# Cross-attention values for all heads at once, memory rows on partitions, and a reordered opening in a two-layer trunk

## The reference, cut to what matters

```
h = rms_norm(x, attn_norm_w[i]); proj = h @ w_in[i]      # xq: 4 heads x 128; cq: 512; gates ...
mh = rms_norm(mem, mem_norm_w[i])
mk, mv = jnp.split(mh @ w_mem_kv[i], 2, axis=-1)         # (256, 4 x 128) each
sc = einsum('bqhd,bkhd->bhqk', xq, mk) * 128 ** -0.5
pc = softmax(sc, axis=-1)
co = einsum('bhqk,bkhd->bqhd', pc, mv)
```

## Time and profile before

| | us |
|---|---|
| median of 3 runs (lowest, highest) | 1961.29 (1961.13, 1962.27) |
| the profiled execution, its own time | 1960.48 |
| its span in the profile | 1958.7 |
| TensorE matmul busy | 1946.5 (99%) |
| GpSimd busy | 1067.7 (55%) |
| VectorE busy | 1038.8 (53%) |
| ScalarE busy | 928.4 (47%) |

### The profile page before, as it was taken

One profiled execution on the slowest core, in us unless ns is written; L12 is line 12 of the kernel. 1 busy time (PEld: TensorE's weight loads), 2 busy tenths in 40 slices (PEclk: granted clock), 3 DMA queues, 4 the chain that ended last, 5 costly groups with the idle time before them and its releaser, 6 DMA issues.

```text
span 1958.7 us, 28631 instructions
## 1 busy us (share of the span) xinstructions
PE 1946.5 (99%) x9308; PEld 1630.4 (83%) x9308; DVE 1038.8 (53%) x1912; ACT 928.4 (47%) x1648; POOL 1067.7 (55%) x1418
## 2 busy tenths in 40 slices
PE   9999999999999999999999999999999999999998
PEld 7888888888888888888888888888888888888887
DVE  6555888887655333321154658888875543333111
ACT  6344666676544222233344456666674342222332
POOL 5555454444555555557765645345445555555674
PEclk9999999999999999999999999999999999999999
DMA  6332222223542322233343322222245332222232
GB/s 248 109 120 87 87 83 90 76 81 137 190 146 86 107 96 96 96 110 96 105 135 121 114 81 92 81 79 89 89 162 185 116 101 94 99 96 94 82 93 91
DMA packets 117938, 212.62 MB, mean 109 GB/s; under 512 B 14290, under 2 KB 31698, under 8 KB 117332
## 3 DMA queue, kind: packets, MB, share of 16 engines
q1 hardware_dynamic: 100944, 176.47, 27.5%
q10 hardware_dynamic: 16900, 34.92, 5.0%
HBM read 194.03 MB, written 17.31 MB: 108 GB/s over the span
## 4 chain that ended last, share of the span: by engine, by line
PE 99%; DVE 0%; ACT 0%; issue 0%; ACTq 0%
PE proj L601 24%; PE proj L603 24%; PE proj L602 24%; PE score L601 2%; PE score L602 2%; PE score L603 2%; PE flip L674 2%; PE score L656 2%; PE score L834 1%; PE score L836 1%; PE score L660 1%; PE score L659 1%; PE att L582 1%; PE att L583 1%; PE att L581 1%; PE score L848 1%
## 5 line engine op out<-in xcount | busy, mean ns | idle before, releaser
L558 POOL TENSOR_TENSOR w_lo<-raw,w_hi 128x256 fp32r<-128x256 f32 x1372 | 1062.6, 807 | 869.5 <-ACT w_hi L1125 869.4
L601 PE MATMUL proj<-h_hi,w_hi 128*128 128x512 f32 x1568 | 619.6, 395 | 0.0
L603 PE MATMUL proj<-h_hi,w_lo 128*128 128x512 f32 x1568 | 612.2, 390 | 0.0
L602 PE MATMUL proj<-h_lo,w_hi 128*128 128x512 f32 x1568 | 611.1, 390 | 0.0
L1125 ACT ACTIVATE w_hi<-raw 128x1024 fp32r<-128x1024 f32 x344 | 362.4, 1055 | 189.0 <-PE proj L603 55.8
L603 PEld LDWEIGHTS proj<-h_hi,w_lo 128*128 128x128 f32 x1568 | 294.4, 188 | 62.4
L602 PEld LDWEIGHTS proj<-h_lo,w_hi 128*128 128x128 f32 x1568 | 294.8, 188 | 58.3
L601 PEld LDWEIGHTS proj<-h_hi,w_hi 128*128 128x128 f32 x1568 | 294.7, 188 | 58.4 <-issue 0.6
L601 PE MATMUL proj<-hid_hi,w_hi 128*128 128x512 f32 x330 | 129.1, 391 | 0.0
L603 PE MATMUL proj<-hid_hi,w_lo 128*128 128x512 f32 x330 | 128.6, 390 | 0.0
L602 PE MATMUL proj<-hid_lo,w_hi 128*128 128x512 f32 x330 | 128.5, 389 | 0.0
(11 more groups left out here) (410 smaller groups left out, 3149.7 us busy)
## 6 DMA issues: line engine op xcount, KB each, us to landing
raw<-in_w_in SPq DMA_DIRECT2D x224, 256.0 KB, 2.8
raw<-in_w_gate_up SPq DMA_DIRECT2D x176, 256.0 KB, 2.8
raw<-in_w_down SPq DMA_DIRECT2D x96, 192.0 KB, 2.4
gate_in<-gate_scratch ACTq DMA_DIRECT2D x48, 256.0 KB, 4.2
gate_scratch<-gate_out ACTq DMA_DIRECT2D x46, 256.0 KB, 2.0
raw<-in_w_mem_kv SPq DMA_DIRECT2D x32, 256.0 KB, 2.8
raw<-in_w_o_diff SPq DMA_DIRECT2D x32, 256.0 KB, 2.8
raw<-in_w_out SPq DMA_DIRECT2D x32, 256.0 KB, 2.8
```

Of the source, the lines that this page charges most:

```text
L558: ins = g.tensor_tensor(w_lo[s][:, cols], raw[s % 2][:, cols], w_hi[s][:, cols].bitcast(F32), ALU.subtract)
L601: mm(o, hi[:, c:c + width], rh, start=start and k == 0, stop=False)
L602: mm(o, hi[:, c:c + width], rl, start=False, stop=False)
L603: ins = mm(o, lo[:, c:c + width], rh, start=False, stop=stop and k == n - 1)
```

## The change

- The memory values of all four heads are computed at once: `memory_values` takes 128 memory rows of `mem_hi` or `mem_lo` as the stationary operand and a slot of 2 x 512 weight columns as the moving one, 12 matmuls of 512 columns for each of four slots. Results gather in two banks, `att` and `score[2]`. The transposes of the values (`flip_memory`), `v_mem`, `v_hi` and `v_lo` of the cross steps are gone.
- The four value slots are N4, N5 and, in the first cross step (now stage Y with 5 slots), Y1 and Y3. Y is xq, values, keys, values, cq. The later steps (stage C) have 3 slots: xq, keys, cq, with `cross_attend` behind cq. A layer has as many slots as before.
- When the last value slot is done, ScalarE writes `cv_hi` (2 x 128x512, scaled by `mem_root`) and VectorE `cv_lo`.
- Opening: the memory tiles `mem_hi` come ahead of the sines; no diagonal matrices, `x_root` and `mem_root` are broadcast as the stationary operand against the identity; `spread_x` stands inside N3 (before: inside N4).
- VectorE: `cross_out` comes after `cq_raw`, `q_sum` and `rope_rows`.
- The cross steps are written out in place of loops on ScalarE and SyncE. `w_mem_kv` is passed as two arrays, keys and values.

```diff
-        SLOTS = dict(N=(5, 1), C=(4, CROSS - 1), A=(6, 1), ...
+        value_bank = [att, score[2]]
+        SLOTS = dict(N=(6, 1), Y=(5, 1), C=(3, CROSS - 2), A=(6, 1), ...
...
+        def of_step(i, k):
+            return ("C", i - 1, k) if i else ("Y", 0, (0, 2, 4)[k])
...
             def cross_slots(l, i):
-                slot(l, "C", i, 0, *whole(w_in, l, i + (T_XQ + 1)))
-                slot(l, "C", i, 1, *whole(w_mem_kv, l, i + 1))
-                slot(l, "C", i, 2, *whole(w_mem_kv, l, i + (CROSS + 1)))
-                slot(l, "C", i, 3, *whole(w_in, l, i + (T_CQ + 1)))
+                slot(l, *of_step(i, 0), *whole(w_in, l, i + (T_XQ + 1)))
+                if i == 0:
+                    slot(l, "Y", 0, 1, *memory_values(l, 2))
+                slot(l, *of_step(i, 1), *whole(w_mem_k, l, i + 1))
+                if i == 0:
+                    slot(l, "Y", 0, 3, *memory_values(l, 3))
+                slot(l, *of_step(i, 2), *whole(w_in, l, i + (T_CQ + 1)))
...
+            def memory_values(l, c, stage, s):
+                w = ring(stage, s)
+                pe.wait_ge(slot_lo.sem, slot_lo.at(l, stage, 0, s + 1))
+                if c == 0:
+                    pe.wait_ge(att_read.sem, att_read.at(l, "C"))
+                    if l:
+                        pe.wait_ge(rstd_done.sem, rstd_done.at(l, "N1", 0, 1))
+                for k in range(2 * c, 2 * c + 2):
+                    m = slice(k % 2 * CROSS * P, (k % 2 + 1) * CROSS * P)
+                    for t in range(NM):
+                        rows, o = slice(t * P, (t + 1) * P), value_bank[t][:, :]
+                        mm(o, mem_hi[:, k, rows], w_hi[w][:, m], start=k == 0, stop=False)
+                        mm(o, mem_hi[:, k, rows], w_lo[w][:, m], start=False, stop=False)
+                        ins = mm(o, mem_lo[:, k, rows], w_hi[w][:, m], start=False, stop=k == KD - 1)
+                ins.then_inc(slot_done.sem, 1)
...
             def spread_x():
-                mm(ssq[:, :], ones[:, :], x_diag[:, :, :].rearrange("p t n -> p (t n)"), start=True, stop=True).then_inc(ssq_full.sem, 1)
+                for t in range(NT):
+                    ins = mm(flip[1][:, t * P:(t + 1) * P], x_root[:, t:t + 1].to_broadcast([P, P]), ident[:, :], start=True, stop=True)
+                ins.then_inc(ssq_full.sem, 1)
...
                 for i in range(CROSS - 1):
                     cross_scores(l, i)
+                    project_xq(l, i)
                     if i == 0:
-                        flip_memory(l, 0)
-                    project_xq(l, i)
-                    project_mem(l, "C", i, 1, 1, (tile_ready, tile_ready.at(l, "C", i + 1)))
+                        memory_values(l, 2, "Y", 1)
+                    project_mem(l, i)
+                    if i == 0:
+                        memory_values(l, 3, "Y", 3)
                     cross_flip(l, i)
-                    project_mem(l, "C", i, 2, 0, (xq_copied, xq_copied.at(l, "C", i + 1, 1)))
+                    project_cq(l, i)
                     cross_attend(l, i)
-                    project_cq(l, i)
-                    flip_memory(l, i + 1)
...
-                with act.Fori(0, CROSS - 1) as i:
+                for i in range(CROSS - 1):
                     cross_step(l, i)
...
-                    split_ahead(l, "C", i, 0)
+                    stage, step, s = of_step(i, 0)
+                    split_ahead(l, stage, step, s, step)
+                    split_ahead(l, stage, step, s + 1, step)
+                    if i == 0:
+                        split_ahead(l, stage, step, 2)
+                        split_ahead(l, stage, step, 3)
+                        values_by_memory(l)
                     cross_high(l, i)
```

More of the change, by code:

```diff
@@ L420, in slot @@
                 assert len(parts) == 2
-                half = ring(stage, s, step if stage == "B" else 0) % 2
+                half = ring(stage, s, step if stage in "BC" else 0) % 2
                 for col, src in parts:
@@ L466, in _ @@
                         sp.dma_start(mem_row[:, t, :], mem_rows[:, t, :]).then_inc(in_mem_row[t], 16)
-                slot(l, "N", 0, 4, *whole(w_mem_kv, l, CROSS))
-                with sp.Fori(0, CROSS - 1) as i:
+                for c in range(2):
+                    slot(l, "N", 0, 4 + c, *memory_values(l, c))
+                for i in range(CROSS - 1):
                     cross_slots(l, i)
@@ L859, in cross_attend @@
             def cross_attend(l, i):
-                pe.wait_ge(flip_read.sem, flip_read.at(l, "C", i, 4))
+                pe.wait_ge(flip_read.sem, flip_read.at(l, "C", i, 2))
                 pe.wait_ge(att_read.sem, att_read.at(l, "C", i))
-                product([(att[:, :], v_hi[:, j, :], v_lo[:, j, :], pt_hi[:, j * SEQ:(j + 1) * SEQ], pt_lo[:, j * SEQ:(j + 1) * SEQ])
+                if i == 0:
+                    pe.wait_ge(cv_split.sem, cv_split.at(l, "N", 0, NM))
+                c = slice(i * P, (i + 1) * P)
@@ L863, in cross_attend @@
+                product([(att[:, :], cv_hi[:, j, c], cv_lo[:, j, c], pt_hi[:, j * SEQ:(j + 1) * SEQ], pt_lo[:, j * SEQ:(j + 1) * SEQ])
                          for j in range(NM)]).then_inc(att_full.sem, 1)
[L865 to L869, removed]
+            def memory_values(l, c, stage, s):
[13 more added lines that the diff above has]
+                ins.then_inc(slot_done.sem, 1)
@@ L1918, in cross_low, with values_by_memory @@
                     s = slice(j * SEQ, (j + 1) * SEQ)
-                    flip_low(l, "C", i, 2 + j, pt_lo[:, s], flip[j][:, :], pt_hi[:, s])
-            def memory_low(l, i):
-                for j in range(NM):
-                    flip_low(l, "C", i, j, v_lo[:, j, :], flip[j][:, 0:P], v_hi[:, j, :])
+                    flip_low(l, "C", i, j, pt_lo[:, s], flip[j][:, :], pt_hi[:, s])
+            def values_by_memory(l):
+                for t in range(NM):
+                    ve.wait_ge(cv_high.sem, cv_high.at(l, "N", 0, t + 1))
+                    v.scalar_tensor_tensor(cv_lo[:, t, :], value_bank[t][:, :], mem_root[:, t:t + 1], cv_hi[:, t, :].bitcast(F32),
+                                           ALU.mult, ALU.subtract).then_inc(cv_split.sem, 1)
             def cross_out(l, i):
@@ L2075, in new_layer @@
                 out_cq(l, 0, "N", 0, 2)
-                out_cross(l, "N", 0, 4, flip[1], v_mem[:, :])
                 if l == 0:
```

127 lines of the change are left out of this document (65 added, 62 removed).

## The result

The changed kernel takes 1966.95 us (median of 11 runs, 1965.16 to 1967.99) where the kernel before takes 1961.90 (11 runs): ratio 1.0027, 95% interval 1.0019 to 1.0036, so 5.05 us slower by the medians, and 3.7 to 7.1 by the interval. Predicted was 1966.3 against a median of 1961.29, +5.0. The profiled execution took 1966.86, span 1965.1 (before 1958.7).

What follows compares the result with a forecast made beforehand. TensorE's own work and its waits were taken to bound the kernel. Terms -3.3 - 1.9 + 4.6 + 0.7 + 2.6 + 1.9 + 0.4 summed to +5.0, from a 1961.29 median to 1966.3 us, range 1961.5 to 1971.

Steps and rivals of the forecast that it cites:

- Less work, -3.3: Memory values, both layers: four units of 2.72 replace four of 2.95 and four transpose pairs, -1.7 us per layer.
- Waits that go, -1.9: Around layer 0's first scores: TensorE's waits for `kT` and `v_mem` go, -1.9 us.
- The opening, +4.6: Opening of layer 0: TensorE waits in N3, before N4, N5 and Y0, +4.6 us, bounds 3.4 and 5.8.
- Y0's wait: Opening of layer 0: slot 6's copy stands behind the square of `cq_raw`, so Y0 waits 1.2 us.
- First cross step, cq +0.7: Layer 0's first cross step: cq waits 0.7 us for slot 10, bounds 0 and 1.3.
- The 7.7 of the loop: Weight-slot loop: 7.7 us from the low half of slot s to that of slot s + 2.
- step 6: Prediction's terms at nothing: loops written out (bounds ±0.5), later steps' supply, `cross_out` order and layer 1's `rstd_done` wait.
- Product +2.6: Layer 0's first cross step: `pt_hi` behind slot 12's copy delays the product 2.6 us, bounds 1.8 to 3.3.
- Layer 1, +1.9: Layer 1's first cross step: the product waits 1.9 us for `pt_lo`, bounds 1.0 and 4.5.
- Rope rows, +0.4: Layer 0, VectorE: rope rows ahead of the maxima delay probabilities, +0.4 us, near the low end of 0 to 1.7.
- The clock: Rival: clock falls in the 2.6 wait, next unit takes 10.9 instead of 5.45, giving 1971.8 us; chance 0.04.
- Supply is quicker: Rival: slot loop turns in some 5.5 us, `cross_attend` never waits, giving 1958.1; chance 0.07 of faster than 1957.4.

Runs made afterwards that it cites:

- the run with ScalarE's order: Against the changed kernel, ScalarE's copy of slot 12 goes behind the value copies and `pt_hi` in both layers' first cross step: 1963.10 us, ratio 1.0010.
- the second profile: Profile of the changed kernel run once more, unchanged: 1966.51 us, ratio 1.0027 to the kernel before.
- the first profile: Profile of the changed kernel's first measurement: profiled execution 1966.86 us, span 1965.1, median 1966.95.
- with the orders mended and the waits filled: Changed kernel with slot 6's and slot 12's copies and rope rows moved, plus 13 transposes hidden in the opening's waits: 1958.74 us, ratio 0.9986.

## Why the prediction was right, step by step

The forecast of +5.0 met 5.05 in the medians, but not by every term, and that it is so near is luck.

1. *Less work, -3.3*: right. In the run with ScalarE's order layer 1 has no wait of the cross part, and from its first scores to its first latent product takes 1089.39 - 1009.91 = 79.48, where before it took 83.67; two value units (5.44) moved ahead of it against 2.88 of the old value unit there, so the layer is 4.2 - 2.6 = 1.6 shorter (forecast 1.7). The Trainium skill's formula for an isolated matmul (page "TensorE: Matmul & The Clock Gate", section "Back-to-back issue gap") would have made it 0.9; the rows (12 matmuls in 2.72, 227 ns each) stay above its 216 ns here too.
2. *Waits that go, -1.9*: right; the scores start at 39.93 without a wait.
3. *The opening, +4.6*: right in place and size: Y0 at 42.79 (forecast 42.8), 42.32 in the second profile. A part of its reason was wrong. I took the reordered sines for 0.75 of it and they were 0.1 to 0.6. And Y0's wait (forecast 1.2, view 0.98) I had rightly derived from the square that stands ahead of slot 6's copy, but without asking whether it must stand there: with the copy moved ahead of the square this wait is gone.
4. *First cross step, cq +0.7*: the step that was mis-sized. It measured 1.9 and 2.5 from start to start. The 7.7 of the loop has some 3 in it for a load to land, and one half of slot 10's took 4.7 to 5.0. In step 6 I had entered the longer code of ScalarE and SyncE at nothing and had not asked when TensorE's own code, which changed too, is fetched. Which of the edits put that fetch into slot 10's load wasn't tried.
   *Product +2.6*: right in mechanism, `pt_lo` done at 67.7 and 66.8 (forecast 66.2); wait 0.46 in the first profile, since cq itself ran late and slow, and 2.17 in the second. *Layer 1, +1.9*: 1.58 and 1.24, within its bounds of 1.0 and up.
5. *Rope rows, +0.4*: they cost nothing. The copies took 0.18 each, GpSimd being idle, and the transposes of step 1 did not wait. Before, with GpSimd at work from 53.14 to 56.09, four of the twelve copies took 0.71 to 0.73, so the choice of the low end was right. When the step became shorter by ScalarE's order the wait appeared (0.89).
6. *The clock*, a rival at 0.04: it fell in both profiles and cost 1.6 to 1.8 there. I had it behind the 2.6 and took a whole unit for its length, 5.4; it was some 3 us at 0.50. The evidence I had was one wait of 0.98 without a fall, which says nothing of a wait of 2.6; with six waits forecast within some 35 us the chance should have been larger.

In the first profile, by the difference from the forecast, cq (+1.8) and the clock (+1.8) stand against the product (-2.1) and the rope rows (-0.4), together the 1.1 by which layer 0 exceeds its forecast; layer 1 met its own within 0.1. So against the profiled execution the sum was 1.4 short (1965.5 forecast, 1966.86 measured); against the medians it was exact, because the profiled execution of before (1960.48) lay 1.4 under its median of 11 runs and that of after at its median. The exact hit is owed to which executions were profiled, and not to the sum. *Supply is quicker*, the rival on the other side, failed: from slot 6 to slot 8 the copies stand 7.5 and 7.8 apart in the two profiles, and still 8.05 apart with slot 6's copy early.

## What to carry to other kernels

In an engine that runs its instructions in order, ask of each instruction that stands behind a copy whether it needs that copy. Two such neighbours (`pt_hi` behind slot 12, slot 6 behind a square) and one late load cost more than the 3.3 us of matmuls that the change saved; with the orders mended and the waits filled the same change is 0.14% faster. And tell the pace of a supply from its start: slots 6 and 8 of layer 0 were copied 7.3 to 8.2 apart in all thirteen profiles of the new form, near the 7.7 read before, but when the first of them was copied hung on one instruction's place. Look for idle time just ahead of it: ScalarE stood idle for 3.92 ahead of the square.

## What the runs showed of the hardware

- **Instruction fetch delays a load.** In ten profiles a 16 KB instruction packet fell into slot 10's load, and one half landed after 3.8 to 5.0 us instead of some 3.0. With 13 more matmuls ahead of it the packet came 2 to 2.5 us earlier, before the load, and both halves landed after 2.8 to 3.3: in three profiles of three. That the packet holds one of the 16 DMA engines and with it the last piece of the load is my reading, not shown. The Trainium skill, page "Runtime: NRT & Kernel Launch", section "Instruction fetch mechanics", says that each sequencer fetches blocks of 16 KiB by its own queue and calls the cost mostly hidden; the packet agrees with it in size, but here slot 10's copy came 1.6 earlier without it, and cq waited for that slot.
- **The clock after a standstill.** In six profiles the granted clock fell to 0.50 for some 3 us in layer 0's first cross step, each time behind a wait there of 2.17, 2.17, 2.17, 2.19, 2.22 or 2.38. Where the waits there were shorter or filled it did not fall. One wait is not the whole of it: in layer 1 of the run with cq ahead of the last value unit TensorE waited 2.38 as well, and the clock stayed at 1.00. One thing that differs there is that no other wait had gone before, while layer 0 had had three to five since 25 us; whether that decides wasn't tried. The page "TensorE: Matmul & The Clock Gate" of the Trainium skill, section "The HAM clock gate (the "warmup" mystery)", has the clock follow how busy the array has been; the traces agree as far as they go.
